# Differential attention: the next head's queries and keys asked for ahead of a store, and lambda computed behind the first row minima

## The reference, cut to what matters

```
def diff_attend(q, k, v, lam):
    s = jnp.einsum('bqhzd,bkhzd->bhzqk', q, k).astype(jnp.float32)
    p = jax.nn.softmax(s, axis=-1)
    a = p[:, :, 0] - lam * p[:, :, 1]
    return jnp.einsum('bhqk,bkhe->bqhe', a.astype(v.dtype), v)
...
lam = jnp.exp(jnp.sum(lq[0] * lk[0])) - jnp.exp(jnp.sum(lq[1] * lk[1])) + lambda_init
```

## Time and profile before

| | us |
|---|---|
| median of 3 timed runs | 2460.21 (2458.68, 2460.21, 2465.53) |
| the profiled execution, its own time | 2453.96 |
| its span | 2452.2 |
| PE busy in the span | 2271.4 (93%) |
| DVE busy | 1117.9 (46%) |
| ACT busy | 991.7 (40%) |
| POOL busy | 883.2 (36%) |
| granted TensorE clock, mean over the span | 0.969 |

### The profile page before, as it was taken

How to read it: one execution, slowest core, us unless ns; L and a number is a source line. 1 busy time by engine, 2 the same in 40 slices (tenths; PEclk the granted TensorE clock), 3 DMA queues, 4 the chain that set the end, 5 groups by cost and what they waited for, 6 DMA issues and landing times. The chain is left out here.

```text
span 2452.2 us, 31971 instructions
## 1 busy us (share of the span) xinstructions
PE 2271.4 (93%) x12292; PEld 1881.7 (77%) x12292; DVE 1117.9 (46%) x1976; ACT 991.7 (40%) x2007; POOL 883.2 (36%) x771
## 2 busy tenths in 40 slices
PE   6999476998999999999999999999999799999797
PEld 5799344886888888888887887888888688888455
DVE  4555475881522222222222535044421788888334
ACT  5434353881522122113113426233321677777432
POOL 4433133453331222123123216322110677777332
PEclk9999687999999999999999999999999999999899
DMA  4365744632111111112011111356646336433322
GB/s 147 97 163 132 225 146 108 177 79 86 39 65 35 48 56 51 36 52 69 26 48 65 56 35 65 112 173 202 190 149 176 97 98 145 119 95 91 124 95 82
DMA packets 202280, 248.47 MB, mean 101 GB/s; under 512 B 63592, under 2 KB 123384, under 8 KB 202128
## 3 DMA queue, kind: packets, MB, share of 16 engines
q1 hardware_dynamic: 196368, 240.14, 33.5%
q10 hardware_dynamic: 5760, 6.29, 0.8%
HBM read 172.88 MB, written 65.10 MB: 97 GB/s over the span
## 5 line engine op out<-in xcount | busy, mean ns | idle before, releaser
L2071 POOL TENSOR_TENSOR rm_w_lo<-rm_stage,rm_w_hi 128x512 fp32r<-128x512 f32 x192 | 247.1, 1302 | 652.1 <-ACT rm_w_hi L2141 651.5
L2141 ACT ACTIVATE rm_w_hi<-rm_stage 128x512 fp32r<-128x512 f32 x192 | 117.9, 626 | 286.0 <-PE rm_down L236 234.0
L236 PE MATMUL rm_down<-rm_w_hi,rm_h_hi 128*128 128x512 f32 x512 | 203.5, 397 | 0.0
L236 PE MATMUL rm_down<-rm_w_lo,rm_h_hi 128*128 128x512 f32 x512 | 202.9, 396 | 0.0
L236 PE MATMUL rm_down<-rm_w_hi,rm_h_lo 128*128 128x512 f32 x512 | 202.8, 396 | 0.0
L2778 DVE TENSOR_REDUCE da_low_score<-da_scores 128x1 f32<-128x1280 f32 x128 | 190.1, 1486 | 26.5 <-PE da_scores L2658 26.4
L2761 POOL TENSOR_TENSOR da_prob<-da_prob 128x1280 f32<-128x1280 f32 x64 | 188.3, 2943 | 5.3
L2329 DVE TENSOR_TENSOR residual<-residual,rm_down 128x512 f32<-128x512 f32 x128 | 87.4, 687 | 225.4 <-PE rm_down L236 224.8
L2719 ACT ACTIVATE da_prob<-da_scores,da_low_score 128x1280 f32<-128x1280 f32 x128 | 170.5, 1332 | 7.4 <-DVE da_low_score L2778 7.3
L2658 PE MATMUL da_scores<-da_k_hi,da_q 128*128 128x512 f32 (+1 forms) x384 | 149.3, 389 | 18.9 <-ACT da_prob L2719 10.7
L2320 DVE TENSOR_TENSOR rm_act_r<-rm_act_r 128x512 f32<-128x512 f32 x64 | 45.5, 711 | 222.3 <-ACT rm_act_r L2184 222.3
(11 more groups left out here) (397 smaller groups left out, 6234.1 us busy)
## 6 DMA issues: line engine op xcount, KB each, us to landing
rm_stage<-in_w_mlp_up SPq DMA_DIRECT2D x64, 256.0 KB, 2.8
rm_stage<-in_w_mlp_down SPq DMA_DIRECT2D x64, 256.0 KB, 2.7
rm_stage<-in_da_w_in SPq DMA_DIRECT2D x64, 256.0 KB, 3.2
gla_ada_w<-in_ada_w SPq DMA_DIRECT2D x12, 1024.0 KB, 7.1
da_k_hi<-dk_hi SPq DMA_DIRECT2D x32, 320.0 KB, 7.7
da_k_lo<-dk_lo SPq DMA_DIRECT2D x32, 320.0 KB, 9.3
dp_swapped<-dp_x SPq DMA_DIRECT2D x128, 64.0 KB, 2.0
da_q<-dq SPq DMA_DIRECT2D x32, 256.0 KB, 6.1
```

The source lines that it names most:

```text
L236: last = nc.tensor.matmul(out, x, y, start=(n == 0), stop=(n == total - 1))
L2071: nc.gpsimd.tensor_tensor(lo, stage[:, n % SLOTS], hi.bitcast(F32), ALU.subtract).then_inc(w_lo_ready, 1)
L2141: nc.scalar.activation(hi, stage[:, n % SLOTS], ACT.Copy).then_inc(w_hi_ready, 1)
```

## The change

Two things are moved; no operation is added or taken away.

1. SP: for the second half of each head up to the sixth, the wait for `scored` and the twelve DMAs for queries and keys of head h + 2 now stand ahead of the wait for `o_added` and the store. The two DMAs for the values stay behind the store.
2. Lambda: its four small operations on DVE now stand in a function, `weight_of_second`, called behind row_min(0, 0) and row_min(0, 1) and ahead of row_min(1, 0). On ACT its exp stands behind exp(0, 0) and exp(0, 1).

```
             for m in range(N // 4):
                 h, half = divmod(m, 2)
-                sp.wait_ge(o_added, 2 * (m + 1))
-                sp.dma_start(d["do"][h, :, half * NCOL:(half + 1) * NCOL], o_sb[:, m % 2]).then_inc(o_stored[m % 2], 16)
                 if half and h + 2 < DH:
                     sp.wait_ge(scored, 2 * QT * (h + 1))
                     c.load_head(sp, d, h + 2, 0, qk_loaded[h % 2])
                     c.load_head(sp, d, h + 2, 1, qk_loaded[h % 2])
+                sp.wait_ge(o_added, 2 * (m + 1))
+                sp.dma_start(d["do"][h, :, half * NCOL:(half + 1) * NCOL], o_sb[:, m % 2]).then_inc(o_stored[m % 2], 16)
+                if half and h + 2 < DH:
                     c.load_values(sp, d, h + 2, v_loaded[h % 2])
...
         def _(act):
...
-            act.wait_ge(lam_summed, 1)
-            nc.scalar.activation(lam_exp[:], lam_sum[:], ACT.Exp).then_inc(lam_exped, 1)
-
...
                 if 0 <= n + 2 < N:
                     exp(n + 2, 1)
+                if n == -2:
+                    act.wait_ge(lam_summed, 1)
+                    nc.scalar.activation(lam_exp[:], lam_sum[:], ACT.Exp).then_inc(lam_exped, 1)
...
         def _(dve):
-            dve.wait_ge(lam_loaded, 32)
...
-            dve.wait_ge(lam_step, 3)
+            def weight_of_second():
...
             for n in STEPS:
                 if 0 <= n + 2 < N:
                     row_min(n + 2, 1)
+                if n == -2:
+                    weight_of_second()
                 if 0 <= n < N:
                     low(n, 0)
```

More of the change, by code:

```diff
@@ L2764, in _, with weight_of_second @@
         def _(dve):
[L2765 to L2774, removed]
+            def weight_of_second():
+                dve.wait_ge(lam_loaded, 32)
+                nc.vector.tensor_tensor(lam_prod[:], lam_in[:, 0], lam_in[:, 1], ALU.mult).then_inc(lam_step, 1)
+                dve.wait_ge(lam_step, 1)
+                nc.vector.tensor_reduce(out=lam_sum[:], in_=lam_prod[:], op=ALU.add, axis=AX.X).then_inc(lam_summed, 1)
+                dve.wait_ge(lam_exped, 1)
+                nc.vector.tensor_tensor(lam[:], lam_exp[:, 1:2], lam_exp[:, 0:1], ALU.subtract).then_inc(lam_step, 1)
+                dve.wait_ge(lam_step, 2)
+                nc.vector.tensor_scalar(lam[:], lam[:], -LAMBDA_INIT, None, ALU.add).then_inc(lam_step, 1)
+                dve.wait_ge(lam_step, 3)
             def row_min(n, z):
```

## The result

| | before | after |
|---|---|---|
| median of 4 timed runs, us | 2460.84 (2458.68 to 2465.53) | 2447.15 (2441.31 to 2448.04) |
| profiled execution, its own time | 2453.96 | 2447.79 |
| its span | 2452.2 | 2446.0 |

The ratio is 0.9924, with a 95% interval of 0.9899 to 0.9948. On 2460 us that is a gain of 18.7 us, between 12.8 and 24.8. The forecast, 2449.3 from 2460.2, was a ratio of 0.9956, a gain of 10.9: the right sign and the right places, and too small. The medians lie 13.7 us apart, the two spans only 6.2. So the first question is where the spans differ. Four instants of each trace tell it: the first scores of the stage, POOL's first and last L2759 (L2760 after), and the first matmul of the stage behind.

What follows compares the result with a forecast made beforehand. PE, busy 93% of the span, was taken to bound the kernel, with waits for keys and exp; -7.2 for the loads and -3.7 for lambda make -10.9 us, from 2460.2 to 2449.3 us, range 2442.5 to 2455.5.

Steps and rivals of the forecast that it cites:

- Part 1: Starts of heads 2 to 7: keys requested 22.4 us earlier, all six PE waits for them go, -7.2 us.
- Part 2: Stage's start: lambda moved behind the first minima, so exp and PE's second row of scores start earlier, -3.7 us.
- the clock's bound: Stage's start: depending on PE's clock in the score rows, lambda's move gains between 2.6 and 4.3 us.
- Another wait in the keys' place: Heads' starts: exp of the row before holds PE instead, leaving only -3.7 us, 2456.5 us; chance 10%.
- The dearer table switch: Stage's start: the exp table switch costs about 1.3 us more in the chain, -9.6 us, 2450.6 us; chance 12%.
- Slower through the clock: Stage's start leaves PE at 1.2 GHz when dense steps begin; with three such steps 2466 us; chance 3%.

Runs made afterwards that it cites:

- loads alone: The kernel before with only the queries and keys loaded ahead of the store, lambda as before; ratio 0.9951, 12.1 us faster.
- the three edits of the start: The changed kernel with the exp table loaded early (ratio 0.9913), with matmuls filling PE's rest behind the first row of scores (0.9933), or with table and two fillings (0.9934).
- the early table: The changed kernel, with ACT computing exp of a constant once the stage's loads are done, so the exp table is there before the first minimum; ratio 0.9913.

## Why the prediction was right and wrong

- **What bounds, and where: right.** The waits for the keys at six heads and the one long wait at the start were the places; nothing else in the stage moved.
- **Part 1, the mechanism: right.** Loads 0.37 us behind the first store, no wait left, no late store, no cost of contention. With the keys early five of six traces (after twice, loads alone, and the three edits of the start) have 63 steps in 348.65 to 348.98 us; the sixth has 349.93, with the low clock of its start in the first step.
- **Part 1, the size: wrong.** This is the term that failed: "7.2 us is what the six waits cost". It was read from one execution, the cheapest of the four that were then seen. The 63 steps take 358.86 us on average before and 348.78 after, so the term is 10.1 us instead of 7.2. Of the 2.7 us by which the mean lies above the first trace, 1.7 is at heads 4 and 7, where the four falls of the clock were, about 1.5 us each, and 0.6 is the longer wait at head 2. The prediction weighed the clock at the start of the stage only; it read the cost from a trace in which no wait for the keys was followed by a fall. It then took the same 7.2 us off the timed median, as if the timed executions waited like the profiled one. It did say that the waits might be other there, and used that for the range, not for the value.
- **Part 2: the chain right, the clock's bound too narrow.** 3.69 was worked out for the chain; the two first profiles gave 3.60 between them, and lambda's wait was covered, by 0.88 us where 0.6 was said. The bounds of 2.6 and 4.3 were for the clock. But to POOL's first it was 10.38 in one trace and 11.45 in the other, 2.3 less than the mean before, below the lower bound: in the second the clock was low in the first row of scores, which the prediction had at full clock. Before, lambda's wait hid such a fall: with the loads alone the clock fell 0.6 us into the first scores, and POOL still began after 13.63 us. By the means the start gained 2.9.
- **Sum.** Means of the stage: 396.11 before, 383.18 after, 12.9 us against 10.9 forecast. That lies in both timed intervals (12.8 to 24.8, and 11.1 to 18.7), at the low end of the first. The 18.7 us of the first ratio are also more than the 17.7 that the range had room for, though the median, 2447.15, lies within it. Whether anything beyond 12.9 exists is open: the executions also differ by some 5 us ahead of the stage, in both kernels.
- **Rivals.** Another wait in the keys' place: out. The dearer table switch: out, by the exp 0.02 us behind the load and the early table's 1.36. Slower through the clock: out; the change removed rests that let the clock fall.

## What to carry to other kernels

Read a wait that a DMA decides from several traces before giving it a number: here the same six waits cost 7.4 to 12.0 us in four executions (their 63 steps, less the 348.78 of the changed kernel), and one profile happened to be the cheapest. Count a rest of PE at its length plus the chance of a stretch at half the clock behind it, and ask for a load when its place is free, not when the next thing in the queue is ready. When timed medians and profiled spans disagree, compare the same stretch between two fixed instructions.

## What the runs showed of the hardware that was not expected

- After rests of PE of only about 2 us (1.82 and 2.19 are two of them) the clock fell in some executions, four times in four traces, with PE already at work again, and came back after about 3.4 us; seven rests of the same length had no fall. With rests of 3.9 to 5.3 us it fell every time, six of six.
- A matmul of the 128x128 fp32 identity by itself took 0.23 us, and is two records in the trace (88 in 10.06 us for 44), twice what had been reckoned from the transposes.
- The same loads, asked for at the same point of the program, made head 2 wait 0.41 to 1.84 us in different executions.
